# Sums of feed-forward weights taken from the pair stretches, made by GpSimd in other stages and kept in HBM

## What is computed

```python
D_FF = -(-8 * D_MODEL // (3 * 256)) * 256          # 2816; D_FF_2 is 2816 too

def hybrid_layer(x, ...):
    ...                                            # mLSTM, dilated attention, merge
    hf = rmsnorm(x, norm_ffn_g)
    x = x + (jax.nn.silu(hf @ w_gate) * (hf @ w_up)) @ w_down

def second_block(x, ...):
    ...                                            # GLA, sparse attention (NSA), merge
        h = rms_norm(x, norm_ffn_pre[l])
        f = (jax.nn.silu(h @ w_ffn_gate[l]) * (h @ w_ffn_up[l])) @ w_ffn_down[l]
        x = x + rms_norm(f, norm_ffn_post[l])
```

## Time and profile before

| | |
|---|---|
| median of three runs | 1911.17 us |
| span of the profiled execution | 1909.1 us |
| PE busy | 1898.5 us (99%) |
| DVE busy | 1255.4 us (66%) |
| ACT busy | 735.3 us (39%) |
| POOL busy | 265.1 us (14%) |
| moved by DMA | 172.77 MB, mean 90 GB/s |
| granted clock of TensorE | 1.000 of full speed |

### The profile page before, as it was taken

The page is one execution under the profiler, slowest core; times in us unless marked ns, Lnnn a source line. Parts: engine busy times, 40 slices in busy tenths (PEclk is TensorE's granted clock), DMA queues, the critical chain, the costliest instruction groups (busy, mean ns, idle before and its releaser), DMA issues.

```text
span 1909.1 us, 26308 instructions
## 1 busy us (share of the span) xinstructions
PE 1898.5 (99%) x10599; PEld 1591.0 (83%) x10599; DVE 1255.4 (66%) x1894; ACT 735.3 (39%) x1265; POOL 265.1 (14%) x156
## 2 busy tenths in 40 slices
PE   9999999999999999999999999999999999999998
PEld 7788888888888888999997778877777878899998
DVE  7777543345455748777776756766776667887874
ACT  6332322233334444344435522224444354444442
POOL 0211210111111113000004001121111133100002
PEclk9999999999999999999999999999999999999999
DMA  5322233232321323233333222322121322333332
GB/s 177 102 70 85 88 86 115 89 99 67 89 67 45 115 91 104 78 106 102 114 108 103 77 67 78 100 79 65 56 67 40 116 79 87 100 100 100 100 130 81
DMA packets 53472, 172.77 MB, mean 90 GB/s; under 512 B 5963, under 2 KB 10643, under 8 KB 53352
## 3 DMA queue, kind: packets, MB, share of 16 engines
q1 hardware_dynamic: 52912, 170.66, 28.8%
q10 hardware_dynamic: 440, 0.44, 0.1%
HBM read 168.86 MB, written 2.22 MB: 90 GB/s over the span
## 4 chain that ended last, share of the span: by engine, by line
PE 94%; DVE 3%; ACT 1%; POOL 1%; issue 0%; DVEq 0%
PE PS L1561 22%; PE PS L1563 22%; PE PS L1562 22%; PE PS L1637 5%; PE PS L1639 5%; PE PS L1638 5%; PE PS L1983 1%; PE PS L2005 1%; PE PS L1780 1%; PE PS L1795 1%; PE PS L1961 1%; PE PS L1841 1%; PE PS L1827 1%; PE PS L1818 1%; PE PS L1748 1%; POOL XT L3338 1%
## 5 line engine op out<-in xcount | busy, mean ns | idle before, releaser
L1561 PE MATMUL PS<-HH,WH 128*128 128x512 f32 x1124 | 444.0, 395 | 0.8 <-DVE WL L2467 0.7
L1563 PE MATMUL PS<-HH,WL 128*128 128x512 f32 x1124 | 438.0, 390 | 0.0
L1562 PE MATMUL PS<-HL,WH 128*128 128x512 f32 x1124 | 437.4, 389 | 0.0
L2064 ACT ACTIVATE WH<-RAW 128x1024 fp32r<-128x1024 f32 (+2 forms) x256 | 261.1, 1020 | 336.4 <-PE PS L1563 271.4
L2467 DVE TENSOR_TENSOR WL<-RAW,WH 128x1024 fp32r<-128x1024 f32 (+2 forms) x195 | 251.2, 1289 | 113.7 <-ACT WH L2064 112.0
L1561 PE MATMUL PS<-AH,WH 128*128 128x512 f32 x816 | 323.7, 397 | 0.0
L1563 PE MATMUL PS<-AH,WL 128*128 128x512 f32 x816 | 318.1, 390 | 0.0
L1562 PE MATMUL PS<-AL,WH 128*128 128x512 f32 x816 | 317.6, 389 | 0.0
L1561 PEld LDWEIGHTS PS<-HH,WH 128*128 128x128 f32 x1124 | 211.1, 188 | 49.7 <-issue 4.2
L1563 PEld LDWEIGHTS PS<-HH,WL 128*128 128x128 f32 x1124 | 211.0, 188 | 45.1
L1562 PEld LDWEIGHTS PS<-HL,WH 128*128 128x128 f32 x1124 | 211.2, 188 | 42.2 <-issue 0.2
(11 more groups left out here) (360 smaller groups left out, 2260.7 us busy)
## 6 DMA issues: line engine op xcount, KB each, us to landing
RAW<-wst SPq DMA_DIRECT2D x292, 512.0 KB, 3.6
RAW<-wst SPq DMA_DIRECT2D x16, 256.0 KB, 2.6
RAW<-wst SPq DMA_DIRECT2D x8, 384.0 KB, 3.1
XT<-xT SPq DMA_DIRECT2D x3, 512.0 KB, 7.3
out<-XT SPq DMA_DIRECT2D x4, 384.0 KB, 2.5
AR<-mx SPq DMA_DIRECT2D x4, 256.0 KB, 6.2
AR<-scr SPq DMA_DIRECT2D x16, 64.0 KB, 4.3
AR<-scr SPq DMA_DIRECT2D x8, 128.0 KB, 4.8
```

What stands on the lines that cost most here:

```text
L1561: T.matmul(out, wh, XH[:, k, :], start=k == 0, stop=False)
L1562: T.matmul(out, wh, XL[:, k, :], start=False, stop=False)
L1563: m = T.matmul(out, wl, XH[:, k, :], start=False, stop=k == nk - 1)
L2064: t = A.activation(whole(WH, i, n), raw(i)[:, 0:n], ACT.Copy, scale=1.0)
```

## The change

The sums of all 28 pairs are no longer made by DVE in the feed-forward layers. POOL makes them in the stages before: those of the first layer's 14 pairs while units 9 to 92 run (mLSTM and attention, one pair every 6 units), those of the second layer's from the unit gv 0 on (GLA and NSA, one pair every 4 units). For each pair SP loads the two raw units into one half of a new buffer SG (1 MB), POOL adds four times 128x512 in place, and SP stores the four sums (1 MB) into a new tensor `sums` in HBM. In the feed-forward layers SP loads the seven chunks of a pair one by one (128x512, 256 KB each), three from the weights and four from `sums`; RAW is now dealt out in six halves, each free when the rest of its last holder is taken. `chunk_hi` waits for its own chunk's load alone. `dynamic_dma_scratch_size` is set to 256.

```diff
 def place_raw():
-    order, user, slot, before = list(range(NR)), {}, {}, {}
+    slot, before, holder, h = {}, {}, [None] * (2 * NR), 0
     for i, (name, j, k0, nk) in enumerate(UNITS):
...
+            pieces = [((i, c), (h + c,), ("lo", i, c)) for c in range(7)]
...
-            user[x] = [("lo", i, 4), ("lo", i, 5), ("added", i, 6)] if p == i else [("lo", p, 2), ("lo", p, 6)]
...
+def sums_ahead():
+    plan = {}
+    for first, period, pairs in ((9, 6, [n for n, i in enumerate(PAIRS) if UNITS[i][0][-1] != "2"]),
+                                 (AT["gv", 0, 0], 4, [n for n, i in enumerate(PAIRS) if UNITS[i][0][-1] == "2"])):
+        for x, n in enumerate(pairs):
+            for step, what in ((0, "load"), (2, "s1"), (3, "s2"), (3, "s4"), (4, "s3"), (5, "store")):
+                plan.setdefault(first + period * x + step, []).append((what, n))
+    return plan
...
 def ahead(e, i):
...
+    for what, n in SUMS_AHEAD.get(i, []):
+        if what == "load":
+            e.sum_load(n)
+        elif what == "store":
+            e.sum_store(n)
+        else:
+            e.sum_add(n, what)
...
-            while n_add < min(n_hi + 2, len(chunks)):
-                e.chunk_add(*chunks[n_add])
-                n_add += 1
...
+            def load_pair(s, i):
+                n = PAIRS.index(i)
+                for c in range(7):
+                    for key in R_BEFORE[i, c]:
+                        sp.wait_ge(*at(*key))
+                    if CHUNKS[c] in SUM_AT:
+                        sp.wait_ge(*at("sum", "stored", n))
+                        o = SUM_AT[CHUNKS[c]]
+                        src = sums_d[n, :, o:o + 512]
+                    else:
+                        o = 0 if CHUNKS[c] == "a11" else 512
+                        src = wst_d[i + (CHUNKS[c] == "a22"), :, o:o + 512]
+                    S.dma_start(raw_chunk(i, c), src).then_inc(*raw_in[R_SLOT[i, c]].next("raw", i, c))
+            def sum_load(s, n):
+                if n > 1:
+                    sp.wait_ge(*at("sum", "stored", n - 2))
+                for x in (0, 1):
+                    d = S.dma_start(SG[:, n % 2, 1024 * x:1024 * x + 1024], wst_d[PAIRS[n] + x, :, :])
+                    d.then_inc(*sum_in[n % 2].next("sum", "raw", n, x))
+            def sum_store(s, n):
+                sp.wait_ge(*at("sum", "s3", n))
+                sp.wait_ge(*at("sum", "s4", n))
+                S.dma_start(sums_d[n, :, :], SG[:, n % 2, :]).then_inc(*sum_out[n % 2].next("sum", "stored", n))
...
             def chunk_hi(s, i, c):
-                act.wait_ge(*(at("raw", i + c // 3) if CHUNKS[c][0] == "a" else at("added", i, c)))
+                act.wait_ge(*at("raw", i, c))
...
-            def chunk_add(s, i, c):
...
-                    dve.wait_ge(*at("raw", i + 1))
-                    t = V.tensor_tensor(r2[:, 0:512], r2[:, 0:512], r2[:, 512:1024], ALU.add)
...
+            def sum_add(s, n, what):
+                g = SG[:, n % 2, :]
+                s2, s4, s1, s3 = (g[:, o:o + 512] for o in (0, 512, 1024, 1536))
+                if what == "s1":
+                    pool.wait_ge(*at("sum", "raw", n, 0))
+                    pool.wait_ge(*at("sum", "raw", n, 1))
+                    t = G.tensor_tensor(s1, s1, s3, ALU.add)
+                elif what == "s2":
+                    pool.wait_ge(*at("sum", "s1", n))
+                    t = G.tensor_tensor(s2, s2, s1, ALU.subtract)
+                else:
+                    pool.wait_ge(*at("sum", "s2", n))
+                    x = s4 if what == "s4" else s3
+                    t = G.tensor_tensor(x, x, s2, ALU.add)
+                t.then_inc(*pool_done["sums"].next("sum", what, n))
```

More of the change, by code:

```diff
@@ L212, in place_raw @@
 def place_raw():
-    order, user, slot, before = list(range(NR)), {}, {}, {}
+    slot, before, holder, h = {}, {}, [None] * (2 * NR), 0
     for i, (name, j, k0, nk) in enumerate(UNITS):
+        p = pair_start(i)
         if name in ("if", "small2"):
             continue
[L219 to L222, removed]
         if p is None:
-            user[x] = [("lo", i)]
-        else:
-            user[x] = [("lo", i, 4), ("lo", i, 5), ("added", i, 6)] if p == i else [("lo", p, 2), ("lo", p, 6)]
+            h += h % 2
+            pieces = [((i, None), (h, h + 1), ("lo", i))]
+        elif p == i:
+            pieces = [((i, c), (h + c,), ("lo", i, c)) for c in range(7)]
+        else:
+            continue
+        for key, at, reader in pieces:
+            at = [x % (2 * NR) for x in at]
+            slot[key] = at[0]
+            before[key] = [x for x in dict.fromkeys(holder[y] for y in at) if x]
+            for x in at:
+                holder[x] = reader
+            h += len(at)
     return slot, before
@@ L231 @@
 R_SLOT, R_BEFORE = place_raw()
+PAIRS = [i for i in range(len(UNITS)) if pair_start(i) == i]
+SUM_AT = {"s2": 0, "s4": 512, "s1": 1024, "s3": 1536}
+def sums_ahead():
[6 more added lines that the diff above has]
+    return plan
+SUMS_AHEAD = sums_ahead()
 class Signal:
@@ L819, in ffn_pairs @@
     forms = [(f, m) for m in range(4) for f in (e.forms_x, e.forms, e.forms_hi, e.forms_lo, e.none)]
-    n_hi, n_add, pending, queue = 0, 0, [], []
+    n_hi, pending, queue = 0, [], []
     for n, (kind, i, x) in enumerate(steps):
@@ L1177, in build @@
         dve_done = {n: signal("dve_" + n) for n in ("norm", "mlstm", "attn", "ffn", "gla", "nsa")}
-        pool_done = {n: signal("pool_" + n) for n in ("norm", "mlstm", "ffn", "gla")}
-        raw_in = [signal(f"raw_in{i}", 16) for i in range(NR)]
+        pool_done = {n: signal("pool_" + n) for n in ("norm", "mlstm", "ffn", "gla", "sums")}
+        raw_in = [signal(f"raw_in{i}", 16) for i in range(2 * NR)]
+        sum_in, sum_out = ([signal(f"{n}{i}", 16) for i in range(2)] for n in ("sum_in", "sum_out"))
         x_in = [signal(f"x_in{i}", 16) for i in range(5)]
@@ L1333, in raw @@
         def raw(i):
-            return RAW[:, R_SLOT[i], :]
+            return RAW[:, R_SLOT[i, None] // 2, :]
         def raw_chunk(i, c):
-            x, o = ((i, 0), (i, 512), (i + 1, 0), (i + 1, 512), (i, 0), (i, 512), (i + 1, 512))[c]
-            return raw(x)[:, o:o + 512]
+            h = R_SLOT[i, c]
+            return RAW[:, h // 2, h % 2 * 512:h % 2 * 512 + 512]
         GATE = parts(18432, 512, 512)
@@ L1463, in load @@
                     return
-                for key in R_BEFORE[i]:
+                p = pair_start(i)
+                if p is not None:
+                    if p == i:
+                        s.load_pair(i)
+                    return
+                for key in R_BEFORE[i, None]:
                     sp.wait_ge(*at(*key))
                 d = S.dma_start(raw(i)[:, 0:nk * 128], wst_d[i, :, 0:nk * 128])
-                d.then_inc(*raw_in[R_SLOT[i]].next("raw", i))
+                d.then_inc(*raw_in[R_SLOT[i, None]].next("raw", i))
+            def load_pair(s, i):
[21 more added lines that the diff above has]
+                S.dma_start(sums_d[n, :, :], SG[:, n % 2, :]).then_inc(*sum_out[n % 2].next("sum", "stored", n))
             def store_vectors(s):
@@ L3535 @@
     mx = nc.dram_tensor("mx", (4, 512), f32, kind="Internal").ap()
-    build(nc, *aps, out, scr, mx)
+    sums = nc.dram_tensor("sums", (len(PAIRS), 128, 2048), f32, kind="Internal").ap()
+    build(nc, *aps, out, scr, mx, sums)
     r = run_bass_kernel_spmd(nc, [arrays], core_ids=[0])
```

25 lines of the change are left out of this document (5 added, 20 removed).

## The result

The changed kernel takes 1916.86 us (median; 1916.77 to 1917.05), the kernel before took 1911.13 us beside it: a ratio of 1.003, interval 1.0018 to 1.0041. That is 5.7 us or 0.3% slower. The time lies in the range, but not in the likeliest case: the forecast was 1912.9 us and "no change" (within 0.2%, up to 1915.0), and 1916.86 us lies above its own upper bound of 1916 too. The profiled execution has a span of 1915.0 us, 5.9 more than before.

What follows compares the result with a forecast made beforehand. PE, busy 1898.5 of 1909.1 us, was taken to bound the kernel. Terms 0 + 0 + 1.2 + 0.5 gave +1.7 us, 1910.8; with 2.1 us up to the median, 1912.9 us; range 1909.5 to 1919.0.

Steps and rivals of the forecast that it cites:

- What bounds the kernel: Whole kernel: PE, busy 1898.5 of 1909.1 us, sets the time; in the pairs relieving DVE gains 0.
- The term of 76.6 us: In the pairs: 28 pairs x 4 adds x 0.684 us taken off DVE, worth 0 on PE's path.
- Pieces: In the pairs: loading chunks in 256 KB pieces costs 0, with 3 us spare on a piece's path.
- Rival (3): In the pairs: pieces land late, from some 5.6 us on PE waits in every pair; 1944 us at 6.6; chance 0.03.
- SP, transfers, POOL's queue: Outside the pairs: SP's longer queue, 56 MB more transfers and rests queued behind POOL's adds cost 0.
- The meeting at 1448: In NSA: POOL's s1 holds DVE's L3117 on a chain without slack, +1.2 us (bounds 0 to 2.4).
- The step that failed: The other ten hit DVE steps in NSA, with GLA and attention: POOL's adds delay them, +0.5 us (0 to 5).
- rival (1): In NSA every meeting of POOL's adds with DVE lands on PE's path, 7.5 us, about 1 elsewhere: 1919.7 us; chance 0.21.
- The prediction's own signs: In the changed profile: DVE near 60% in pairs, POOL 410 to 450 us, NSA waits 1 to 2 us if right.
- Rivals (2): In the pairs: DVE's relief shortens PE's waits or spaces its matmuls closer, under 1907.35 us; chance 0.03.
- rival (4): The change doesn't do what it says: sums late or DVE still adds; time as forecast, no chance of its own.

Runs made afterwards that it cites:

- e4: The changed kernel with nothing made ahead (no SG loads, adds or stores), all seven chunks loaded in pieces from the plain weights: 1911.16 us.
- e1: The changed kernel without POOL's 112 adds, with loads into SG, stores to HBM and pieces kept: 1911.15 us.
- e5: The changed kernel with each of POOL's 112 adds replaced by a memset of 1344 columns, which reads nothing from SBUF: 1911.37 us.
- e8: The changed kernel without the 16 adds of pairs 0, 16, 20 and 27, transfers kept: 1912.65 us.
- e10: The changed kernel with the second layer's loads and stores of sums moved into the first layer's pairs, and its 56 adds left out: 1914.2 us.

## Why the prediction was right or wrong

**What bounds the kernel.** Right. PE's busy time is the same to 0.1 us, its waits decide, and 63.9 us less of DVE's work are worth nothing that can be measured (e4). The term of 76.6 us was itself a bit large, since DVE's records overlap (in the timelines a step of 0.68 us is followed by the next after about 0.60); it hangs on nothing.

**Pieces.** Right: 0 (e4). The landing of a 256 KB piece has gone from 2.6 us to 3.4, out of a bound of 5.6. The changed kernel's issue of the sums (KB each, us to landing), which the other pieces match:

```profile
RAW<-sums SPq DMA_DIRECT2D x112, 256.0 KB, 3.4
```

Rival (3) needed 2.2 us more. Two rates were worked out with 1 MB as 1024 x 1024 bytes and were a little low: 2.36 million bytes in 15.4 us are 153 GB/s and not 146 (152 measured), and the added loads and stores outside the pairs are 56 GB/s and not 53. Nothing hangs on it. DVE's share in the pairs fell from 78 to 67 and 65%; near 60 had been said.

**SP, transfers, POOL's queue.** Right: 0 as far as it can be measured (e1, and e5 for POOL's queue). POOL came to 431.3 us, within 410 to 450.

**The meeting at 1448.** It happened as the order had it, and the size was near: +1.2 us were put there, 1.78 are lost between 1447 and 1462. But only part of it is s1. DVE's row and POOL's in the changed kernel:

```profile
1453.29 1.74 DVE L3155 TENSOR_SCALAR AR<-AR,GT 128x512 f32<-128x512 f32 x2
1452.57 1.72 POOL L3325 TENSOR_TENSOR SG<-SG 128x512 f32<-128x512 f32 x1
```

The two steps take 1.74 us instead of 1.00, +0.74 and not +1.2: HL's step went first and waited out the rest, so s1 had run 0.7 of its 1.7 us when L3155 came. The other 1.0 us came from the adds of pair 26, twenty microseconds ahead (the two make 1.7; PE goes from 4.13 to 5.82 us late there). DVE stood 4.13 us late at 1423.83 (1419.70 before) and 5.10 us late at 1436.89 (1431.79 before), held three times in a row, the first time by a rest and then twice by adds, where one hold of 2.1 us by a rest stood before (L3154, 2.49 us for 0.42):

```profile
1428.35 2.62 DVE L3188 TENSOR_TENSOR AR<-AR,C 128x248 f32<-128x248 f32 x1
1431.01 1.37 DVE L3192 TENSOR_TENSOR AR<-AR 128x248 f32<-128x248 f32 x1
1432.30 1.49 DVE L2790 TENSOR_SCALAR AR<-AR 128x512 f32<-128x512 f32 x1
```

This lateness stayed with DVE until it met the one place without margin. In e8, where pair 27's adds are out and pair 26's in, the two steps take 1.00 us again and PE's starts still shift by 0.96 us there (from 0.63 to 1.59 us late).

**The step that failed** is "For them and for GLA and attention together I take +0.5 us (0 to 5)", with "in mLSTM and GLA ... PE's waits are nearly none and its margins some microseconds". Outside 1447 to 1462 the table shows 0.52 + 0.78 + 1.28 + 1.12 = 3.7 us, and 0.34 at the start. With the 1.78 these make 5.82 for a forecast of 1.7. mLSTM had no term of its own in the sum, though it was named among the places where steps meet. Two things were wrong in it.

- The margins were taken from the absence of waits. A wait says that a margin is 0, its absence says nothing of how large it is. At 1115 us the margin stood in the trace of before as the idle time of the copy behind the scan, 0.55 us. At L2912 it was indeed some 3 us, and that was not enough.
- A meeting was priced as one wait of at most an add. Where DVE has several such steps in a row and POOL several instructions, the engines take turns, and each step pays: three steps 3.8 us at 95 us, four steps 2.6 us at L3106 (8.02 us for 5.39). The scan had not been counted among the steps that wait at all.

The bound of 5 us for this term did hold, and so did the range. The bounds of the whole forecast did not (1910.5 to 1916, 1916.86 measured): the time lies in the range because the range was stretched over rival (1), not because the forecast was near. The prediction's own signs lean the same way. It called itself wrong if PE's waits inside the program left 2 to 8 us; they are 9.1 us, 7.7 without the 1.4 us by the first weights. In NSA, from 1250 to 1480, they rose from 0.6 to 3.1 us, between its 1 to 2 and the 4 of rival (1). As a check of POOL's harmlessness I had set its 32.74 us in NSA against 0.6 us of PE's waits; those were instructions with gaps of 16 and 18 us between them, not four in a row.

**The rivals.** Rival (1) had the right mechanism and was nearer in time (1919.7 us, and 1912.9 for the forecast), but in too narrow a place. In NSA, from 1247 on, 2.9 us were lost, under the 3.8 from which it decides; the rest fell outside NSA, where it had "about 1 us". Its reason, that margins are spent once a first delay has shifted the items against the units, is what pair 26 shows. The rule behind it, that the Trainium skill gives in Perfetto Trace Analysis, section Optimizing Scalar/DVE Operations (moving work from DVE to GpSimd might not help, as they share a port), describes this case, and the trace agrees: 64 us taken from DVE, 38.5 given back by holding, 5.7 paid by PE. The Trainium skill, SBUF — State Buffer, section Who interferes with whom, says that a DVE step with two SBUF inputs contends with a GpSimd instruction that reads SBUF and not with one that only writes; e5 agrees (a scan of 1.22 us beside a memset, 2.29 beside adds). Rivals (2) and (3) are ruled out by e4, rival (4) by the page (DVE has 112 instructions less, POOL 112 more).

## What to carry to other kernels

Before work that reads SBUF goes to POOL, look at each of DVE's runs of steps with SBUF inputs that it will lie beside, and read the margin behind the run (the idle time of the next step that waits for PE), not the list of PE's waits. If it must go there, cut POOL's instructions short: here a quarter of the length took away all of the 5.7 us that can be measured, though POOL worked 85 us longer. And where one engine is full all the time, ask what work taken from another can be worth at all: here 63.9 us of it were worth nothing.

## What the runs showed of the hardware that was not expected

- The two engines alternate: a waiting DVE step goes when POOL's instruction is done, even if POOL's next one is ready, and that one starts behind it. So n steps beside a full POOL queue take n of POOL's instructions (95.82: three steps in 6.17 us; 1235.41: four in 8.02).
- `tensor_tensor_scan` of 128x512 waits like `tensor_tensor` (1.22 us alone, 2.29 beside adds, 1.48 beside adds of a quarter).
- A memset on POOL holds up neither a scan nor the rest ahead of it (1.22 us each), but it does hold up a `tensor_scalar` from SBUF (eight of them 7.8 us for 4.0).
- An add of 128x128 on POOL takes 0.46 us in the median and one of 128x512 1.30. With those that wait for DVE, the means are 0.59 and 1.50 us, and the 112 adds take 252 us of POOL's time in quarters and 168 whole: half more, and the held steps of DVE wait far less.
- Beside 274 GB/s of transfers PE still is busy 223.72 of 224 us, as long as POOL makes no adds (e10), though by its starts it falls back by 0.8 us in this window, and loads of 512 KB take 6.3 us to landing there for 3.6.
